# A trunk of attention, recurrence and experts: pass count loaded in VectorE's loop, low parts moved to GpSimd, one pair's low parts behind a norm

## The chip, the cores and the metric

The kernel runs on one core of a Trainium2 chip, as one program. TensorE multiplies, VectorE (DVE) and ScalarE (ACT) work element by element, GpSimd (POOL) does small work and some transfers, and SyncE (SP) issues the weight transfers. The metric is the device time of one execution in microseconds.

## The reference

Two decoder layers on 256 tokens of width 1024, all in float32. Layer 0 mixes the tokens with 16-head latent attention (query rank 384, key and value rank 256) and ends with a dense SwiGLU of width 3584. Layer 1 mixes them with a gated linear recurrence and ends with 8 SwiGLU experts, of which each token uses its best two. In front of each part stands an RMS norm, and one behind the last. Cut to what the change touches:

```python
o = softmax(mask(q @ k.T * scale)) @ v        # 16 heads, 2 blocks of 128 queries
h = h + o @ w_o                               # output projection, 1024 x 1024
...
top_val, top_idx = lax.top_k(logits, 2)       # router of 8 experts
y = sum(gate * swiglu(x, w_gate[e], w_up[e], w_down[e]) for the two experts e)
h = rmsnorm(h + y, norm_final)
```

## The kernel before

The program writes one stream of instructions for each engine, in an order fixed by hand, and joins them by semaphores. An engine works its own stream in order, so an instruction that waits holds all behind it.

**Split products.** Up to the recurrence, a matrix product is three TensorE products: each operand is a high part (rounded, in `w_hi`) and a low part (the rest, in `w_lo`), and high times high, low times high and high times low are summed (`product`, lines 424 to 426). Weights come in units of 128 x 2048 into six slots. For each unit ScalarE makes the high parts (`split_hi`, line 398) and another engine subtracts them from the raw weights (`split_lo`, line 404: two inputs and one output in SBUF). The output projection of the attention has four units, `W_O` to `W_O + 3`; TensorE multiplies by them at the end of the heads. In the dense layer GpSimd makes the low parts of one slot in six, one unit in each step.

**The heads.** Scores, softmax and values of the 16 heads are software-pipelined: a loop over `i` writes, on each engine, the stages of several heads. TensorE transposes head `i` (line 1234), multiplies the scores of head `i - 1` (1245, 1246), transposes the probabilities of head `i - 4` (1255) and multiplies pairs of heads by the values (1270, 1274). Score product `h` waits for the maxima of head `h - 2`, since two banks alternate. VectorE does in step `i`: the norm of head `i - 3` (`normalize`, lines 1892 to 1894: a reciprocal and two multiplications in SBUF), the maxima of head `i - 1` (`maxima`, 1883, one operand in PSUM and one in SBUF, and at the end a 128 x 2 multiplication in SBUF, 1886, which raises `max_ready`), in odd steps from 7 on the low parts of a pair of heads (`o_low`, 1899), and in steps 1 and 4 a copy of keys and values (`kv_copy`, 1871 and 1872). In step 1 it also makes the low parts of unit `W_O + 3`, between the maxima of head 0 and a copy. ScalarE copies transposed heads and probabilities (791), makes the exponentials (880) and the high parts of the pairs. GpSimd's last work before the heads end is two copies of rotated keys (711); then it waits for `heads_over`.

**The experts.** The router's plan gives a number of passes over the experts, 1 to 3 by how many tokens the fullest expert has; with these inputs it is 1. VectorE computes it into `n_pass_i` (line 2197, raising `plan_ready`), and each engine loads it into a register and loops `n_pass` times over the experts. TensorE gathers the first expert's tokens (1506) and runs some filler products (1132), VectorE copies them from PSUM in two halves (`xg_copy`, 2212), and TensorE begins the expert's products (1500) when the first half is there. A loop body is entered once before the count is compared at its end.

Of the kernel before, what the change touches and what calls it, by code (L numbers as in the profile page):

```python
# [21 lines left out]
def trunk(nc, x, positions, norm_mix, norm_ffn, norm_final, mla_w_in, mla_q_norm, mla_kv_norm,  # L22
# [10 lines left out]
    HEADS, V = 16, 64  # L33
# [14 lines left out]
    with ExitStack() as ctx:  # L48
        def sb(stack, name, shape, dt):
            return stack.enter_context(nc.sbuf_tensor(name, shape, dt))  # L50

        def sem(name):
            return ctx.enter_context(nc.semaphore(name))
# [14 lines left out]
        n_pass_i = sb(ctx, "n_pass_i", [1, 1], I32)  # L68
# [137 lines left out]
        def mla_use(n):  # L206
            return n % SLOTS, n // SLOTS + 1
# [101 lines left out]
        plan_ready = sem("plan_ready")  # L309
# [44 lines left out]
        W_IN, W_UQ, W_UKV, W_O = 0, 3, 6, 8  # L354
# [45 lines left out]
        def split_lo(eng, use, width=UNIT):  # L400

            s, n = use
            eng.wait_ge(hi_done[s], n)
            eng.tensor_tensor(w_lo[:, s, 0:width], raw[:, s, 0:width], w_hi[:, s, 0:width].bitcast(F32),  # L404
                              ALU.subtract).then_inc(lo_done[s], 1)
# [228 lines left out]
        def _(pool):  # L634
# [75 lines left out]
            for t in range(TT):  # L710
                pool.tensor_copy(k[:, t, :, NOPE:QK],
                                 latent[:, t, QR + KVR:LAT].unsqueeze(1).broadcast_to([P, HEADS, ROPE])
                                 ).then_inc(qk_ready, 1)

            pool.wait_ge(heads_over, 1)
            gain(2, gain_ffn[:], norm_ffn[0])
# [41 lines left out]
            n_pass = pool.value_load(n_pass_i[0:1, 0:1], min_val=1, max_val=3)  # L758
# [948 lines left out]
        def _(dve):  # L1707
# [3 lines left out]
            def link(ins):  # L1711

                links[0] += 1
                ins.then_inc(link_s, 1)
                dve.wait_ge(link_s, links[0])
                return ins
# [147 lines left out]
            def kv_copy(n):  # L1864
                t, b = KV_ORDER[n]
                if n == len(KV_ORDER) - 1:
                    dve.wait_ge(used[mla_use(W_O - 1)[0]], mla_use(W_O - 1)[1])
                else:
                    dve.wait_ge(kv_ps, n + 1)
                src = psum[:, KV_BANKS[t][b]].rearrange("p (h c) -> p h c", h=4)  # L1870
                dve.tensor_copy(k[:, t, 4 * b:4 * b + 4, 0:NOPE], src[:, :, 0:NOPE]).then_inc(kv_copied_v, 1)
                dve.tensor_copy(v[:, t, 4 * b * V:4 * (b + 1) * V].rearrange("p (h c) -> p h c", h=4),
                                src[:, :, NOPE:NOPE + V]).then_inc(kv_copied_v, 1)


            def maxima(h):

                b = h % 4
                dve.wait_ge(score_ps, h + 1)
                if h >= 4:  # L1880
                    dve.wait_ge(probsT_ps, h - 3)
                for r, (c0, c1) in enumerate([(0, P), (P, 3 * P)]):
                    link(dve.tensor_tensor_reduce(probs[:, b, c0:c1], psum[:, 2 + h % 2, c0:c1],  # L1883
                                                  mask[:, 2 * P - (c1 - c0):2 * P], 1.0,
                                                  -BIG, ALU.add, ALU.max, mx[:, 2 * b + r:2 * b + r + 1]))
                dve.tensor_scalar(nmx[:, 2 * b:2 * b + 2], mx[:, 2 * b:2 * b + 2], -SCALE, None,
                                  ALU.mult).then_inc(max_ready, 1)

            def normalize(h):
                b = h % 4  # L1890
                dve.wait_ge(exp_ready, 2 * h + 2)
                link(dve.reciprocal(inv[:, 2 * b:2 * b + 2], tot[:, 2 * b:2 * b + 2]))
                link(dve.tensor_scalar(probs[:, b, 0:P], probs[:, b, 0:P], inv[:, 2 * b:2 * b + 1], None, ALU.mult))
                dve.tensor_scalar(probs[:, b, P:3 * P], probs[:, b, P:3 * P], inv[:, 2 * b + 1:2 * b + 2], None,
                                  ALU.mult).then_inc(probs_ready, 1)

            def o_low(g):
                dve.wait_ge(o_hi, g + 1)
                dve.tensor_tensor(xTl_mla[:, g, :], psum[:, 6 + g % 2, 0:T], xTh_mla[:, g, :].bitcast(F32),
                                  ALU.subtract).then_inc(o_lo, 1)  # L1900

            for i in range(HEADS + 7):
                if 0 <= i - 3 < HEADS:
                    normalize(i - 3)
                if i == 4:
                    kv_copy(KV_SCALAR + 1)
                if 0 <= i - 1 < HEADS:
                    maxima(i - 1)
                if i == 1:
                    split_lo(dve, mla_use(W_O + 3))  # L1910
                    kv_copy(KV_SCALAR)
                if i >= 7 and i % 2 == 1:
                    o_low((i - 7) // 2)

            dve.wait_ge(o_ps, HEADS // 2)
# [281 lines left out]
            dve.scalar_tensor_tensor(out=n_pass_i[:], in0=rs[0:1, 6, 0:1], scalar=2 * FULL, in1=rs[0:1, 6, 1:2],  # L2197
                                     op0=ALU.is_gt, op1=ALU.add).then_inc(plan_ready, 1)

            dve.wait_ge(plan_ready, 1)  # L2200
            n_pass = dve.value_load(n_pass_i[0:1, 0:1], min_val=1, max_val=3)

            def last_one_hot():
                for t in range(TT):
# [3 lines left out]
            def xg_copy(p):  # L2208

                for h in range(2):  # L2210
                    dve.wait_ge(xg_ps, 2 * p + h + 1)
                    dve.tensor_copy(xg[:, 4 * h:4 * h + 4, :], psum[:, BANK_T[h], 0:4 * SLOT_TOKENS].rearrange(  # L2212
                        "p (a b) -> p a b", b=SLOT_TOKENS)).then_inc((xg_half, xg_v)[h], 1)
# [57 lines left out]
            def choice_difference(p):  # L2271

                then(dve.tensor_scalar(rt[:, 2], rt[:, 5], 0.0, None, ALU.is_equal), p)
                then(dve.tensor_scalar(rt[:, 4], rt[:, 5], 1.0, None, ALU.is_equal), p)
                then(dve.tensor_tensor(rt[:, 3], rt[:, 4], rt[:, 2], ALU.subtract), p)
                then(dve.tensor_tensor(rt[:, 1], rt[:, 3], rt[:, 0], ALU.mult), p)
                then(dve.tensor_reduce(rs[:, 2], rt[:, 1], AX, ALU.add), p)
                dve.wait_ge(rstd_ready, MOE_ROOTS + TT)
                dve.tensor_tensor(rs[:, 2], rs[:, 2], rstd[:, 0:TT], ALU.mult).then_inc(top_diff, 1)
# [40 lines left out]
            def sums(n):  # L2320

                dve.wait_ge(main_ready, n * 6 + 6)
                dve.wait_ge(freed, n * UNITS + leaves((None, STEPS - 1, 0)))
                for d in range(2):
                    half_sum(d)
# [14 lines left out]
            def expert(p, e, e_next, to_xg, first=False, last=False):  # L2340
                n = p * E + e
                for m in range(4):
                    if m == 1 and not first:

                        dve.wait_ge(y_stored, p * 16 * (E - 1) + e * 16 + 48)
                        sums(n - 1)
                    if m == 1 and first:
                        choice_difference(p)
                        find_rows(p)
                    if m == 2 and first:  # L2350
                        gates(p)
                    silu(n, m)
                    if m == 3 and not last:
                        transpose_tokens_of(p, e_next, to_xg).then_inc(xg_v, 1)
                    if m == 3 and last:
                        add_rows(p)
                    for h in range(WIDTH[m]):
                        times_up(n, m, h, first)
                        transpose_hidden(n, m, h)
                    if m == 0 and last:  # L2360
                        last_one_hot()
                        transpose_onehot(p)

            with dve.Fori(0, n_pass) as p:
                xg_copy(p)
                expert(p, 0, 1, xg_odd, first=True)
                with dve.Fori(0, (E - 2) // 2) as h:
                    expert(p, h * 2 + 1, h * 2 + 2, xg)
                    expert(p, h * 2 + 2, h * 2 + 3, xg_odd)
                expert(p, E - 1, None, None, last=True)  # L2370

                dve.wait_ge(ohT_ready, p + 1)
                dve.tensor_scalar(key[:], key[:], -FULL, None, ALU.add).then_inc(pass_over, 1)
                dve.wait_ge(pass_over, p + 1)
                for t in range(TT):
                    first_one_hot(t)

                dve.wait_ge(y_stored, p * 16 * (E - 1) + (64 + 16 * (E - 1)))
                last_sums(p * E + (E - 1), p)
                dve.wait_ge(added, p * 8 + 8)  # L2380
                for i, (d, t) in enumerate([(d, t) for d in range(2) for t in range(TT)]):
                    add_result(p, i, t, d)
                dve.wait_ge(added, p * 8 + 12)
# [37 lines left out]
```

## Time and profile before

| | us |
|---|---|
| median of 3 runs | 1317.88 |
| lowest and highest run | 1317.78, 1318.0 |
| the profiled execution | 1318.05 |
| its span, first to last instruction | 1316.2 |
| TensorE busy in the span | 1305.8 |
| VectorE busy | 642.5 |
| ScalarE busy | 283.2 |
| GpSimd busy | 86.9 |

The span is what the trace covers; the execution's own time is 1.85 us longer. All times of the trace are microseconds from the start of the span. A matmul's end is modelled, so that consecutive matmuls overlap in the rows. "Busy" leaves out register work, branches and waits; in the chain of waits the sequencers' own work stands under names such as DVEq.

### The profile page before, as it was taken

The numbers are of one execution on the slowest core, as the hardware profiler recorded it, in microseconds if no ns is written. First come the engines' busy times: TensorE is split into PE (matmuls) and PEld (weight loads), VectorE is DVE, ScalarE is ACT, GpSimd is POOL, SyncE is SP. The second block draws the span as 40 slices with busy tenths as digits, with TensorE's granted clock in tenths as the row PEclk, the third lists the DMA queues.
The fourth block names the chain that finished last, engine by engine and source line by source line (L and its number), as shares of the span: only waits on it lengthen the run. The fifth ranks groups of instructions, "written<-read, shape, count | busy, mean of one in ns | idle before, by whom it ended". The sixth has DMA issues, their size and how long they took to land.

```text
span 1316.2 us, 25501 instructions
## 1 busy us (share of the span) xinstructions
PE 1305.8 (99%) x10922; PEld 768.1 (58%) x10922; DVE 642.5 (49%) x1458; ACT 283.2 (22%) x424; POOL 86.9 (7%) x114
## 2 busy tenths in 40 slices
PE   9999999999999999999999999999999999999998
PEld 5778888888896544444444444444444444444444
DVE  5978666666776253432533523323353353342436
ACT  4874333333584100010010010001001001000102
POOL 2401111111001100000000000000000000000100
PEclk9999999999999999999999999999999999999999
DMA  7815555556467899999999999999999999999992
GB/s 278 306 61 179 193 191 191 191 191 203 153 250 307 314 412 403 420 410 413 420 420 405 418 420 408 419 412 408 408 420 409 407 420 419 406 400 420 419 415 90
DMA packets 124227, 441.92 MB, mean 336 GB/s; under 512 B 7294, under 2 KB 17600, under 8 KB 109536
## 3 DMA queue, kind: packets, MB, share of 16 engines
q1 hardware_dynamic: 119488, 424.57, 81.9%
q0 software_dynamic: 4624, 15.87, 3.3%
q8 instruction: 82, 1.34, 0.4%
q14 instruction: 17, 0.14, 0.0%
q10 hardware_dynamic: 16, 0.00, 0.0%
HBM read 430.84 MB, written 9.57 MB: 335 GB/s over the span
## 4 chain that ended last, share of the span: by engine, by line
PE 95%; DVE 2%; ACT 1%; DMA 1%; issue 0%; SPq 0%; DVEq 0%; POOL 0%
PE psum L1500 66%; PE psum L424 8%; PE psum L426 8%; PE psum L425 8%; DMA raw<-in_mla_w_uq 1%; PE psum L1473 1%; DVE w_lo L404 1%; PE psum L1506 0%; ACT res L880 0%; PE psum L1147 0%; PE psum L1348 0%; ACT gain_mla L791 0%; PE psum L440 0%; DVE res L1883 0%; ACT early L791 0%
## 5 line engine op out<-in xcount | busy, mean ns | idle before, releaser
L1500 PE MATMUL psum<-raw_more,hT 128*32 128x512 f32 x1656 | 535.7, 592 | 0.0
L1500 PE MATMUL psum<-raw,hT 128*32 128x512 f32 x1032 | 334.8, 592 | 0.0
L1500 PE MATMUL psum<-raw_more,xg_odd 128*32 128x512 f32 x1680 | 245.4, 592 | 0.0
L1500 PE MATMUL psum<-raw_more,xg 128*32 128x512 f32 x1704 | 241.8, 592 | 0.7 <-DVE xg L2212 0.7
L1500 PEld LDWEIGHTS psum<-raw_more,hT 128*32 128x32 f32 x1656 | 146.8, 109 | 122.6 <-issue 122.6
L2248 DVE STREAM_TRANSPOSE hT<-hid 32x128 f32<-32x128 f32 x672 | 204.9, 305 | 10.3
L2238 DVE SCALAR_TENSOR_TENSOR hid<-hid,psum 96x512 f32<-96x512 f32 x55 | 37.6, 684 | 303.3 <-PE psum L1500 302.5
L1092 ACT ACTIVATE hid<-psum 96x1024 f32<-96x1024 f32 (+1 forms) x32 | 29.2, 912 | 664.8 <-PE psum L1500 475.8
L1500 PE MATMUL psum<-raw,xg_odd 128*32 128x512 f32 x1008 | 147.7, 592 | 0.0
L1500 PE MATMUL psum<-raw,xg 128*32 128x512 f32 x984 | 144.2, 592 | 0.0
L1500 PEld LDWEIGHTS psum<-raw,hT 128*32 128x32 f32 x1032 | 91.1, 109 | 76.0 <-issue 75.8
L404 DVE TENSOR_TENSOR w_lo<-raw,w_hi 128x2048 fp32r<-128x2048 f32 (+1 forms) x53 | 119.6, 2276 | 30.6 <-ACT w_hi L398 30.5
L2225 DVE SCALAR_TENSOR_TENSOR hid<-hid,psum 96x1024 f32<-96x1024 f32 (+1 forms) x32 | 34.7, 1084 | 201.8 <-ACT hid L1092 201.8
L1500 PEld LDWEIGHTS psum<-raw_more,xg 128*32 128x32 f32 x1704 | 83.4, 110 | 83.5 <-issue 83.5
L1500 PEld LDWEIGHTS psum<-raw_more,xg_odd 128*32 128x32 f32 x1680 | 84.5, 110 | 77.9 <-issue 77.9
L398 ACT ACTIVATE w_hi<-raw 128x2048 fp32r<-128x2048 f32 (+1 forms) x60 | 111.4, 1889 | 19.4 <-PE psum L426 16.7
L424 PE MATMUL psum<-w_hi,xTh_ffn 128*128 128x512 f32 x224 | 87.3, 390 | 0.0
L426 PE MATMUL psum<-w_hi,xTl_ffn 128*128 128x512 f32 x224 | 87.2, 389 | 0.0
L425 PE MATMUL psum<-w_lo,xTh_ffn 128*128 128x512 f32 x224 | 87.2, 389 | 0.0
L1500 PEld LDWEIGHTS psum<-raw,xg_odd 128*32 128x32 f32 x1008 | 50.7, 110 | 46.8 <-issue 46.8
L1500 PEld LDWEIGHTS psum<-raw,xg 128*32 128x32 f32 x984 | 49.5, 110 | 47.9 <-issue 47.9
L791 ACT ACTIVATE y_main<-psum 32x512 f32<-32x512 f32 x48 | 28.4, 592 | 145.1 <-PE psum L1500 145.1
(318 smaller groups left out, 1343.7 us busy)
## 6 DMA issues: line engine op xcount, KB each, us to landing
raw_more<-in_moe_w_gate SPq DMA_DIRECT2D x71, 1024.0 KB, 16.2
raw_more<-in_moe_w_up SPq DMA_DIRECT2D x70, 1024.0 KB, 15.8
raw_more<-in_moe_w_down SPq DMA_DIRECT2D x69, 1024.0 KB, 16.8
raw<-in_moe_w_down SPq DMA_DIRECT2D x43, 1024.0 KB, 16.8
raw<-in_moe_w_up SPq DMA_DIRECT2D x42, 1024.0 KB, 16.2
raw<-in_moe_w_gate SPq DMA_DIRECT2D x41, 1024.0 KB, 17.2
raw<-in_ffn_w_gate SPq DMA_DIRECT2D x14, 1024.0 KB, 5.1
raw<-in_ffn_w_up SPq DMA_DIRECT2D x14, 1024.0 KB, 5.5
```

The lines of the kernel that those rows point to most:

```text
L398: act.activation(w_hi[:, s, 0:width], raw[:, s, 0:width], ACT.Copy).then_inc(hi_done[s], 1)
L404: eng.tensor_tensor(w_lo[:, s, 0:width], raw[:, s, 0:width], w_hi[:, s, 0:width].bitcast(F32), ALU.subtract).then_inc(lo_done[s], 1)
L424: pe.matmul(out_ap, sh, mh, start=first, stop=False, **lone)
L425: pe.matmul(out_ap, sh, ml, start=False, stop=False, **lone)
L426: mm = pe.matmul(out_ap, sl, mh, start=False, stop=last, **lone)
L791: return act.activation(dst, src, ACT.Copy)
L1092: act.activation(hid[:, 0:WIDTH[m] * BANK].rearrange("p (a b) -> p a b", b=BANK), psum[SLOT_ROWS, 0:WIDTH[m]], ACT.Tanh, scale=0.5).then_i ...
L1473: mm = pe.matmul(psum[rows_q, 2 * t + b], states[:, a, c0:c0 + 32], unit(raw, s, D)[:, a % 2, b * BANK:(b + 1) * BANK], start=a == 0, stop ...
L1500: return pe.matmul(psum[rows_q, bank, cols], stationary, moving, start=start, stop=stop, tile_position=(0, rows_q.start), skip_group_check ...
L2225: dve.scalar_tensor_tensor(out=h, in0=h, scalar=1.0, in1=psum[SLOT_ROWS, 0:WIDTH[m]], op0=ALU.add, op1=ALU.mult).then_inc(m_mid, 1)
L2238: dve.scalar_tensor_tensor(out=hid[:, cols], in0=hid[:, cols], scalar=0.5, in1=psum[SLOT_ROWS, BANK_U[h]], op0=ALU.mult, op1=ALU.mult).the ...
L2248: ins = dve.transpose(hT[QUARTERS[to], H_BUF[j], :, QUARTERS[b]].rearrange("p (h r) s -> p h r s", r=2), hid[QUARTERS[b], h * BANK:(h + 1) ...
```

## The change

It has three parts. VectorE no longer loads the pass count ahead of its loop; the wait for the plan and the load stand inside the loop, behind the two token copies, and the range check of the value is left out. The low parts of unit `W_O + 3` are made by GpSimd behind its key copies and not by VectorE in step 1. And `o_low` of pair 4, until now at the end of step 15, stands in step 16 between the norm of head 13 and the maxima of head 15; the other pairs stay where they were.

```diff
--- before.py
+++ after.py
@@ -711,6 +711,8 @@
                 pool.tensor_copy(k[:, t, :, NOPE:QK],
                                  latent[:, t, QR + KVR:LAT].unsqueeze(1).broadcast_to([P, HEADS, ROPE])
                                  ).then_inc(qk_ready, 1)
+
+            split_lo(pool, mla_use(W_O + 3))
 
             pool.wait_ge(heads_over, 1)
             gain(2, gain_ffn[:], norm_ffn[0])
@@ -1902,14 +1904,17 @@
             for i in range(HEADS + 7):
                 if 0 <= i - 3 < HEADS:
                     normalize(i - 3)
+                if i == HEADS:
+                    o_low((HEADS - 1 - 7) // 2)
                 if i == 4:
                     kv_copy(KV_SCALAR + 1)
                 if 0 <= i - 1 < HEADS:
                     maxima(i - 1)
                 if i == 1:
-                    split_lo(dve, mla_use(W_O + 3))
                     kv_copy(KV_SCALAR)
-                if i >= 7 and i % 2 == 1:
+                if 7 <= i < HEADS - 1 and i % 2 == 1:
+                    o_low((i - 7) // 2)
+                if i > HEADS and i % 2 == 1:
                     o_low((i - 7) // 2)
 
             dve.wait_ge(o_ps, HEADS // 2)
@@ -2197,8 +2202,7 @@
             dve.scalar_tensor_tensor(out=n_pass_i[:], in0=rs[0:1, 6, 0:1], scalar=2 * FULL, in1=rs[0:1, 6, 1:2],
                                      op0=ALU.is_gt, op1=ALU.add).then_inc(plan_ready, 1)
 
-            dve.wait_ge(plan_ready, 1)
-            n_pass = dve.value_load(n_pass_i[0:1, 0:1], min_val=1, max_val=3)
+            pass_count = dve.alloc_register("pass_count")
 
             def last_one_hot():
                 for t in range(TT):
@@ -2361,8 +2365,10 @@
                         last_one_hot()
                         transpose_onehot(p)
 
-            with dve.Fori(0, n_pass) as p:
+            with dve.Fori(0, pass_count) as p:
                 xg_copy(p)
+                dve.wait_ge(plan_ready, 1)
+                dve.reg_load(pass_count, n_pass_i[0:1, 0:1])
                 expert(p, 0, 1, xg_odd, first=True)
                 with dve.Fori(0, (E - 2) // 2) as h:
                     expert(p, h * 2 + 1, h * 2 + 2, xg)
```

## Rows read from the trace of the kernel before

**Rows 1.** The page, busy time of TensorE; and its granted clock in 40 slices.

```profile
PE 1305.8 (99%) x10922; PEld 768.1 (58%) x10922; DVE 642.5 (49%) x1458; ACT 283.2 (22%) x424; POOL 86.9 (7%) x114
...
PEclk9999999999999999999999999999999999999999
```

**Rows 2.** The waits of TensorE: for whom; us in total, times, longest us.

```profile
PE psum L1245 <- DVE res L1886: 0.9, 1, 0.9
...
PE psum L1500 <- DVE xg L2212: 0.7, 1, 0.7
```

**Rows 3.** The chain of waits, 52 to 62 us: start, us, what.

```profile
54.22 2.19 DVE w_lo L404
...
58.11 0.46 PE psum L1245 x2
```

**Rows 4.** The chain of waits, 78 to 92 us.

```profile
83.61 0.42 DVE xTl_mla L1899
...
84.88 0.55 PE psum L1255 x3
```

**Rows 5.** The chain of waits, 428 to 446 us.

```profile
435.90 1.15 DVEq L2201
...
437.61 0.57 DVE xg L2212
438.18 0.34 issue
```

**Rows 6.** The timeline of VectorE: start, us, instruction, count; idle time before it.

```profile
46.04 0.85 DVE L1855 TENSOR_TENSOR q<-gain_mla 128x256 f32<-128x256 f32 x1
...
54.05 0.17 DVE L1886 TENSOR_SCALAR res<-res 128x2 f32<-128x2 f32 x1
...
56.33 0.42 DVE L1871 COPY k<-psum 128x256 f32<-128x256 f32 x1
...
57.00 0.28 DVE L1883 CUSTOM_DVE_ANT_0 res<-psum,mask 128x128 f32<-128x128 f32 x1
...
57.32 0.42 DVE L1883 CUSTOM_DVE_ANT_0 res<-psum,mask 128x256 f32<-128x256 f32 x1
...
58.06 0.29 DVE L1893 TENSOR_SCALAR res<-res 128x128 f32<-128x128 f32 x1
58.38 0.35 DVE L1894 TENSOR_SCALAR res<-res 128x256 f32<-128x256 f32 x1
...
86.12 0.35 DVE L1894 TENSOR_SCALAR res<-res 128x256 f32<-128x256 f32 x1
...
156.08 0.69 DVE L1971 SCALAR_TENSOR_TENSOR hid_f<-hid_f,psum 128x512 f32<-128x512 f32 x1 [4.12 <-PE psum L426]
```

**Rows 7.** The timeline of GpSimd (POOL).

```profile
36.13 2.33 POOL L697 TENSOR_TENSOR res<-k,res 128x16 f32<-128x16 f32 x1
...
45.81 0.81 POOL L696 TENSOR_TENSOR k<-q,trig 128x256 f32<-128x256 f32 x1
...
153.12 4.62 POOL L404 TENSOR_TENSOR w_lo<-raw,w_hi 128x2048 fp32r<-128x2048 f32 x1 [26.19 <-ACT w_hi L398]
```

**Rows 8.** The timeline of ScalarE (ACT).

```profile
51.79 1.91 ACT L398 ACTIVATE w_hi<-raw 128x2048 fp32r<-128x2048 f32 x1
...
151.13 1.91 ACT L398 ACTIVATE w_hi<-raw 128x2048 fp32r<-128x2048 f32 x1
```

**Rows 9.** The timeline of TensorE (PE).

```profile
86.66 0.49 PE L1255 MATMUL psum<-ident,res 128*128 128x128 f32 x3
...
435.47 2.02 PE L1506 MATMUL psum<-onehot,xn_moe 128*128 128x96 f32 x16
437.38 0.39 PE L1132 MATMUL psum<-zeros 128*128 128x128 bf16 x4
```

**Rows 10.** Line 1697, TensorE's loop: duration ns min/median/max, first and last start us.

```profile
L1697 PEldq FUSED_REGOPS  x1: 41/41/41, 437.5 to 437.5; - x1
```

**Rows 11.** The timeline of VectorE in the first expert.

```profile
453.55 1.22 DVE L2225 SCALAR_TENSOR_TENSOR hid<-hid,psum 96x1024 f32<-96x1024 f32 x1 [14.92 <-ACT hid L1092]
```

## The prediction

> **What bounds the kernel now.** I read the page's busy times first [rows 1]: TensorE is busy for 99% of the span, so an edit elsewhere counts only where TensorE waits for it. The list of TensorE's waits comes next. It is short, and two entries touch the change [rows 2]: 0.9 us for a VectorE operation of line 1886, and 0.7 us for the token copies of line 2212. The chain of waits then says what stands behind each. In the attention it runs through VectorE from the low parts of the last output-weight unit (54.22, 2.19 us) by the value copies and the second head's maxima to the score product of head 3 at 58.11 [rows 3]. At the end of the heads it runs through `o_low(4)` (83.61, 0.42 us) and the norm of head 13 to TensorE at 84.88, and from there on TensorE works without a gap [rows 4]. Before the expert loop it runs through VectorE's load of the pass count (435.90, 1.15 us) and the first token copy (437.61) to the first expert product, 0.34 us behind the copy [rows 5]. These are the three places edited; the rest is TensorE's own stream, which moves as a block.
>
> **Part A, the pass count.** Removed ahead of the copies: the load, 1.15 us, and the range check behind it, some 0.3 us. The copies then wait for the gather products alone. These 16 records, starting at 435.47, take 2.02 us, to 437.49 [rows 9], so the half that the first copy needs is done about 436.5; the copy takes 0.57 us [rows 5] and ends about 437.1 instead of 438.18. Next late is TensorE itself: its four filler products reach to 437.77 [rows 9], and its own load of the count and loop entry occupy its sequencer until 437.5 [rows 10]. The 0.34 us of issue between copy and product I take as sequencer work on waits; placed behind 437.54 it gives a start at 437.88 instead of 438.52, a gain of 0.64. The most it can be is the wait itself, 0.74 us [rows 5, 9]; the least is nothing. I take 0.65. The second copy is due 0.57 us later, and the product that needs it stands four weight tiles behind the first, so it does not hold. Inside the loop the wait and the load come behind the copies; queued behind them is the first `silu`, which starts only at 453.55 after 14.92 us of idleness [rows 11]. So the load costs nothing there; without that cover it would cost its 1.15 us again. No DMA is issued or moved, and the counts of the other queues are as they were.
>
> **Part B, the low parts on GpSimd.** VectorE loses one operation, 2.19 us on the chain. What that can give is limited by TensorE's wait behind it, 0.9 us [rows 2, 3]: with the maxima of head 1 early, the score product of head 3 starts when the transposes in front of it are done. On GpSimd the same operation takes 4.62 us [rows 7]. GpSimd is idle then and waits for ScalarE's high parts, which end at 51.79 + 1.91 = 53.70 [rows 8]. In the dense layer GpSimd starts 0.08 us behind such an end (151.13 + 1.91 against 153.12 [rows 7, 8]), so here it runs from 53.78 to 58.40. The consumer is TensorE in the output projection, after 90 us, and the slot's next load is a dense weight with tens of microseconds to spare; neither waits. GpSimd's next operation is a load of a gain behind the end of the heads.
>
> The cost is in what VectorE can do in those 4.62 us. The trace shows the two engines shutting each other out: a GpSimd operation of 16 columns took 2.33 us at 36.13, beside VectorE's subtractions, where one of 256 columns takes 0.81, and VectorE's operation of line 1855 took 0.85 us at 46.04, ending 0.27 us behind GpSimd's operation, which ran until 46.62 [rows 7, 6]. Both sides wait for a whole instruction of the other. Not every VectorE instruction is caught: at 156.08, inside a GpSimd split of 4.62 us, one with an operand in PSUM took its ordinary 0.69 us [rows 6]. So the maxima and value copies, which read PSUM, go on. The open question is the single-input operation from SBUF to SBUF. `normalize` takes 0.29 us for 128 columns and 0.35 for 256, so 128 more cost some 0.07 us, where the maxima's cost 0.14 (0.28 and 0.42) [rows 6]: it handles two elements in the time of one, as if it read and wrote by two paths. The operation that ends each head's maxima, line 1886, is of the same kind, with two columns. It is issued at 54.05 [rows 6], 0.27 us behind GpSimd's start. If it is shut out, it ends some 0.1 us behind 58.40, and everything queued behind it on VectorE waits with it: ScalarE's exponentials of head 0, TensorE's score product of head 2, the value copies, the maxima of head 1. From the first value copy at 56.33 to TensorE's start at 58.11 it is 1.78 us now [rows 3, 6]; from 58.48 that leads to 60.26, 2.15 us later than before. TensorE's order behind that point (score product, an up-projection, fillers, transposes) has no gap to absorb it. Bounds: from a gain of 0.9 (nothing is shut out) to a loss of 2.15. I take the loss of 2.15, because the nearest operation of this kind in the trace runs at the doubled rate and both kinds of exclusion that can be seen are total.
>
> The Trainium skill ("SBUF — State Buffer", Who interferes with whom) states that VectorE's second port pair is GpSimd's too, locked for a whole instruction, and that `tensor_scalar` takes it when it runs in a two-port mode; the condition ("VectorE: DVE Perf Modes", Mode 2×_2P) is both sides in SBUF and an even outermost dimension, and no least size is named. By that rule the two-column operation is held and the sum is the one below; if only operations long enough to profit took the port, it would be the first rival. No row here shows the small operation beside a GpSimd instruction.
>
> **Part C, the order at the last heads.** `o_low(4)` moves from in front of the norm of head 13 to behind it. The chain loses 0.42 us there, and TensorE's wait would let it pass. But VectorE's total up to the norm of head 14 is unchanged: it ends at 86.12 + 0.35 = 86.47 [rows 6]. TensorE's transposes of that head started at 86.66, behind a product and not behind VectorE [rows 9]; 0.42 us earlier they would now wait for the norm, until about 86.5. So 0.15 us is left. Ends: 0 and 0.42. The product that reads `o_low(4)` comes two heads later. I take 0.15.
>
> **Sum.** +2.15 - 0.65 - 0.15 = +1.35 us. The profiled execution took 1318.05 us (span 1316.2 and 1.85 around it), so 1319.4; it lies 0.17 above the median of the runs, 1317.88, so in the terms of that median 1319.2.
>
> **Rivals.**
> 1. The two-column operation passes, only the norms are shut out. Head 0's norm, started at 58.06 before, gets its turn at 58.40, and VectorE's queue is 0.34 us later than now behind it, which eats part of the 0.9 us: B is -0.7 (ends -0.9 and -0.55), the sum -1.5, the time 1316.4. For it: a two-column operation gains nothing from the second path. Against it: the norms' rate.
> 2. Nothing single-input is shut out. B is -0.9, the sum with A and C -1.7 to -2.1, the time 1316.0. For it: no row shows such an operation held.
> 3. The first line-1886 operation slips in ahead of GpSimd's start, the second is held to 58.40 and ends at about 58.57, so that TensorE starts near 58.7 instead of 58.11: B +0.6, the sum -0.2, the time 1317.7. It needs GpSimd 0.27 us later than the dense layer's rows say.
> 4. The other side, slower by a measurable amount: with VectorE held, TensorE stands idle most of 56 to 60 us, and its granted clock, 1.00 in every slice of the page [rows 1], falls to its lower level of 1.2 GHz. TensorE's work behind the hold would take twice its time until the clock is back; if that lasts as long as the hold, 4.35 us from 54.05 to 58.40, half of it is lost, 2.2 us, and the time 1321.4. It decides from 1.3 us upward. Against it: there is a score product and a set of transposes inside the hold.
> That the count is loaded too late to do its work in the loop can't be: it is read only at the end of the pass.
>
> **How the numbers follow.** What a measurement of this kernel can tell from no change is about 0.2%, 2.6 us. Likeliest case 0.50, 1319.2, with its own range 1318.6 to 1320.0 (A between 0 and 0.74, C between 0 and 0.42). Rival 1: 0.17. Rival 2: 0.17. Rival 3: 0.08. Rival 4: 0.08. The range from 1315.6 to 1320.2 takes in all but rival 4 and the ends. Faster than 1315.2 needs all three gains at their ends and more: 0.04. Slower than 1320.5 is rival 4 and the case's own upper end: 0.09. The rest, 0.87, is within 0.2%.
>
> **What the changed profile would show.** GpSimd's split at 53.8 for 4.6 us; the first line-1886 operation as one of some 4.4 us instead of 0.17, or, by rival 1, line 1893 at 56.7 with some 1.7 us and line 1886 short; TensorE's score product of head 3 at 60.3 (57.2 by rivals 1 and 2). No `TENSOR_LOAD` of VectorE between the gather and the first copy, and TensorE's wait there gone or under 0.1 us. `o_low` of pair 4 behind the norm of head 13, TensorE's wait for line 1894 shorter. The prediction is wrong if VectorE keeps its short operations beside GpSimd's split, or if TensorE's clock falls.

## The result, and the profile after

The changed kernel takes 1320.39 us (median of 18 runs, 1319.32 to 1322.05), the kernel before 1318.01 (18 runs, 1317.18 to 1321.86). The ratio is 1.0019, with a 95% interval of 1.0012 to 1.0025: 2.4 us slower. The forecast was 1319.2 with a range up to 1320.2, so the time lies just outside of it. The profiled execution took 1319.79 us, its span is 1317.9.

The first rows are of the page of the changed kernel; the one on TensorE's clock shows nothing, since a slice is 33 us wide and a 9 stands for anything from 0.90 up.

```profile
PE 1308.6 (99%) x10922; PEld 770.2 (58%) x10922; DVE 642.6 (49%) x1457; ACT 283.5 (22%) x424; POOL 91.5 (7%) x115
...
PEclk9999999999999999999999999999999999999999
```

TensorE's waits in the changed kernel (us in total, times, longest us), to be read against [rows 2]. Line numbers have moved by two: 1888 is now the end of the maxima, 1247 the score product, 1257 the transposes of the probabilities.

```profile
PE psum L1247 <- DVE res L1888: 2.3, 1, 2.3
...
PE psum L1257 <- DVE res L1896: 0.3, 1, 0.3
PE psum L1502 <- issue: 0.2, 1, 0.2
```

TensorE's wait for the maxima was 0.9 us, at head 3's score product for the maxima of head 1. It is now 2.3 us, and stands one head earlier: at head 2's score product, for the maxima of head 0. The wait for the token copies is gone; 0.2 us of issue stand in its place. Why the first grew is in the timelines of GpSimd and VectorE:

```profile
53.00 4.52 POOL L404 TENSOR_TENSOR w_lo<-raw,w_hi 128x2048 fp32r<-128x2048 f32 x1 [4.79 <-ACT w_hi L398]
```

```profile
53.26 4.29 DVE L1888 TENSOR_SCALAR res<-res 128x2 f32<-128x2 f32 x1
57.46 0.41 DVE L1873 COPY k<-psum 128x256 f32<-128x256 f32 x1
...
58.91 0.17 DVE L1888 TENSOR_SCALAR res<-res 128x2 f32<-128x2 f32 x1
...
59.18 0.29 DVE L1895 TENSOR_SCALAR res<-res 128x128 f32<-128x128 f32 x1
```

GpSimd's split starts at 53.00 and ends at 57.52. VectorE issues the two-column operation at 53.26 and completes it at 57.55: 4.29 us for work that took 0.17 [rows 6]. The value copies behind it, with their input in PSUM, start at once afterwards, and the norm of head 0 (59.18, 0.29 us) finds GpSimd done. TensorE in the same stretch:

```profile
54.97 0.38 PE L1236 MATMUL psum<-ident,k 128*96 128x128 f32 x2
57.69 0.46 PE L1247 MATMUL psum<-gain_mla 96*128 96x128 f32 x2 [2.34 <-DVE res L1888]
...
59.23 0.77 PE L1247 MATMUL psum<-gain_mla 96*128 96x128 f32 x2
...
60.28 0.99 PE L424 MATMUL psum<-w_hi,xTh_mla 128*128 128x512 f32 x1
61.07 0.63 PE L425 MATMUL psum<-w_lo,xTh_mla 128*128 128x512 f32 x1
...
62.21 0.40 PE L425 MATMUL psum<-w_lo,xTh_mla 128*128 128x512 f32 x1
...
63.03 0.50 PE L1257 MATMUL psum<-ident,res 128*128 128x128 f32 x3
```

It is idle from 55.35 to 57.69. Then the products themselves are slow: the one at 60.28 takes 0.99 us and the next 0.63, against 0.40 for the same kind at 62.21. The table by microsecond says why (length, busy us of each engine, then the granted clock, then DMA):

```profile
56.00:57.00 1.00, 0.00 (x0) 0.00 (x0) 1.00 (x1) 0.00 (x0) 1.00 (x1) 1.00 0.95 377
...
58.00:59.00 1.00, 1.00 (x8) 0.76 (x6) 0.93 (x7) 1.00 (x4) 0.00 (x0) 0.81 0.89 123
59.00:60.00 1.00, 1.00 (x5) 0.81 (x4) 0.93 (x6) 0.94 (x5) 0.00 (x0) 0.50 0.63 221
...
61.00:62.00 1.00, 1.00 (x4) 0.73 (x3) 0.47 (x2) 0.00 (x0) 0.00 (x0) 0.50 0.83 340
62.00:63.00 1.00, 1.00 (x10) 0.68 (x9) 0.12 (x1) 0.00 (x0) 0.00 (x0) 0.99 0.06 16
```

The granted clock is 0.81 in the slice from 58 us, 0.50 (TensorE's lower level, 1.2 GHz) from 59 to 62, and 0.99 in the next. It fell after TensorE had been idle for the whole of the microsecond from 56 and most of the two beside it, and was back at 62, with TensorE at work since 57.69. In the trace of the kernel before, with 0.87 us of idleness in this place, the granted clock is 1.00 in each microsecond from 54 to 64. Nor is one trace alone in this: the mean clock of the span is below 1.000 in 17 of the 18 runs of the changed kernel, and in 2 of the 78 runs of the kernel before that were made beside the experiments. In this trace the stage comes 0.79 us earlier than in that of before (the two-column operation is issued at 53.26 and not at 54.05), so the stage is best measured from that issue: head 3's score product follows 5.97 us behind it (before 4.06), and the first transposes of probabilities (63.03) 3.80 us behind the score product (before 60.57 - 58.11 = 2.46). The hold costs 1.91 us, the slow clock 1.34.

The chain of waits at the last heads answers to [rows 4], and before the experts to [rows 5]; VectorE's timeline there stands below.

```profile
88.45 0.36 DVE res L1896
...
88.86 0.55 PE psum L1257 x3
```

```profile
437.83 1.90 PE psum L1508 x16
439.73 0.29 PE psum L1134 x4
440.01 0.23 issue
440.24 5.77 PE psum L1502 x50
```

```profile
438.87 0.56 DVE L2216 COPY xg<-psum 128x384 f32<-128x384 f32 x1 [0.78 <-PE psum L1508]
439.77 0.56 DVE L2216 COPY xg<-psum 128x384 f32<-128x384 f32 x1 [0.34 <-PE psum L1508]
455.27 1.22 DVE L2229 SCALAR_TENSOR_TENSOR hid<-hid,psum 96x1024 f32<-96x1024 f32 x1 [14.95 <-ACT hid L1094]
```

The norm of head 14 now ends the wait at 88.86, as forecast. Before the experts VectorE's load has left the chain: it runs through gather, fillers and 0.23 us of issue to the product at 440.24. The copies start at 438.87 and 439.77, each as its half of the gather is ready, and VectorE's next operation comes at 455.27, so the load behind them (1.14 us at 439.8) is hidden.

### The profile page after: what moved, and what is told of

It is laid out like the page before. It is cut to its first block, busy times and chain, and to the rows that moved or that the text cites. A ratio compares the mean times of both kernels' runs of the same rounds, so it can differ in the third digit from the quotient of the medians.

```text
span 1317.9 us, 25499 instructions
## 1 busy us (share of the span) xinstructions
PE 1308.6 (99%) x10922; PEld 770.2 (58%) x10922; DVE 642.6 (49%) x1457; ACT 283.5 (22%) x424; POOL 91.5 (7%) x115
## 3 DMA queue, kind: packets, MB, share of 16 engines
q8 instruction: 82, 1.34, 0.4%
## 4 chain that ended last, share of the span: by engine, by line
PE 96%; DVE 2%; ACT 1%; issue 0%; DMA 0%; POOL 0%; POOLq 0%; DVEq 0%
PE psum L1502 66%; PE psum L424 8%; PE psum L425 8%; PE psum L426 8%; PE psum L1149 1%; PE psum L1475 1%; PE psum L1508 1%; DMA q<-in_positions 0%; DVE w_lo L404 0%; DVE res L1888 0%; ACT res L882 0%; POOL k L653 0%; PE psum L1350 0%; ACT gain_mla L793 0%; PE psum L440 0%
```

## The experiments

All are compared with the kernel before by 8 to 11 executions of theirs and 15 to 33 of its own; the interval of each ratio is about 0.0009 to either side, so that it tells 1.2 us but not 0.2. Parts of that size are read from the traces, by the distances between five marks that no noise of the start-up reaches: the issue of the first two-column operation (M), the first transposes of probabilities (T), the last 256-column products of the heads by the values (V), the first of the last 16 gather products (G) and the first expert product (X). V to G is 345.66 to 345.68 us in all eleven traces, and X to the end 877.64 to 877.73. A distance comes from one trace of each kernel, but kernels with the same code in a stretch agree there: T-V is 29.19 to 29.22 us in before, A alone and B alone, and M-T 6.50 to 6.52 us wherever VectorE kept the split in step 1. Only G-X scatters more, 2.38 to 2.54 us in the eight kernels with part A. The mark M itself moves from 52.93 to 54.74 us from trace to trace, and what moves it is left out of the sums.

```
kernel        median us  ratio   M-T   T-V    G-X   sum against before
before        1317.9     1       6.52  29.22  3.05
changed       1320.39    1.0019  9.77  29.01  2.54  +2.53
A alone       1317.81    0.9998  6.51  29.21  2.46  -0.61
B alone       1321.46    1.0028  9.76  29.19  3.05  +3.21
C alone       1317.66    1.0000  6.51  29.03  3.04  -0.21
A and C       1316.91    0.9997  6.50  29.03  2.54  -0.72
fillers       1319.14    1.0008  8.45  29.03  2.38  +1.07
one column    1316.01    0.9986  5.42  29.25  2.48  -1.64
odd norm      1316.95    0.9992  5.42  30.03  2.49  -0.85
pieces        1316.53    0.9994  5.86  29.02  2.44  -1.47
late split    1316.11    0.9984  5.41  29.03  2.38  -1.97
```

(Each ratio is to runs of the kernel before made beside those of the other; these had medians of 1317.66 to 1318.21 us, and the table shows a middle one. A ratio differs from the quotient of two medians by up to 0.0004.)

**One part at a time.** My theory was that the parts add up and that all of the loss is B's: hold and clock. The rival put some of it on A or C, or on their sum.

```diff
 # A alone
-            dve.wait_ge(plan_ready, 1)
-            n_pass = dve.value_load(n_pass_i[0:1, 0:1], min_val=1, max_val=3)
+            pass_count = dve.alloc_register("pass_count")
...
-            with dve.Fori(0, n_pass) as p:
+            with dve.Fori(0, pass_count) as p:
                 xg_copy(p)
+                dve.wait_ge(plan_ready, 1)
+                dve.reg_load(pass_count, n_pass_i[0:1, 0:1])
```

> Part A alone (count loaded in the loop), the rest as before. Theory (the three parts add up, and A is worth what TensorE waited for the copies): the first expert product starts 0.64 us earlier behind the gather (before: 438.52 - 435.47 = 3.05 us from the first gather product to it; here 2.4), and the time is 0.05% below before. Rival (the move of code costs something of its own in the loop, and is part of the loss of the whole change): the same distance is 3.0 us or the expert part is longer than before, ratio 1.000 or above.

The distance G-X fell from 3.05 to 2.46 us, 0.59 us, and the expert part is as long as before. The ratio is 0.9998 (0.9989 to 1.0007). The size is the theory's; the ratio by itself is also compatible with nothing.

```diff
 # B alone
+            split_lo(pool, mla_use(W_O + 3))
             pool.wait_ge(heads_over, 1)
...
-                    split_lo(dve, mla_use(W_O + 3))
                     kv_copy(KV_SCALAR)
```

> Part B alone (low parts of the last output-weight unit on GpSimd), the rest as before. Theory (the loss is all B's: a two-column operation held for 4.3 us, about 2.0 us, and the clock that falls behind it, about 1.3 us): the two-column operation takes 4.3 us, the granted clock is below 1.00 between 56 and 64 us, ratio 1.0022 to 1.0028, about 3.2 us above before. Rival (only the hold is B's, the rest is from A or C or their sum): ratio 1.0010 to 1.0016, clock 1.00.

VectorE's operation and the granted clock in this kernel:

```profile
53.45 4.28 DVE L1888 TENSOR_SCALAR res<-res 128x2 f32<-128x2 f32 x1
```

```profile
56.00:60.00 4.00, 2.12 (x11) 1.71 (x12) 3.86 (x12) 2.17 (x8) 1.71 (x1) 0.85 0.64 201
60.00:64.00 4.00, 4.00 (x23) 3.21 (x23) 2.50 (x13) 1.02 (x4) 0.00 (x0) 0.72 0.52 210
```

The hold is there (4.28 us) and so is the clock (0.85 and 0.72), the ratio is 1.0028 (1.0018 to 1.0039), and the distances give 3.21 us. The rival falls.

```diff
 # C alone
                     normalize(i - 3)
+                if i == HEADS:
+                    o_low((HEADS - 1 - 7) // 2)
...
-                if i >= 7 and i % 2 == 1:
+                if 7 <= i < HEADS - 1 and i % 2 == 1:
                     o_low((i - 7) // 2)
+                if i > HEADS and i % 2 == 1:
+                    o_low((i - 7) // 2)
```

> Part C alone (o_low of pair 4 behind the norm of head 13), the rest as before. Theory: TensorE's wait for the norm of head 13 (0.77 us) shrinks to about 0.35, 0.2 us is kept behind the norm of head 14, ratio 0.9998, not to be told from 1. Rival (it is worth the 0.42 us that leaves the chain): the transposes behind the norm of head 14 start 0.4 us earlier, ratio 0.9997. The trace tells them apart, the ratio doesn't.

TensorE's wait for the norm of head 13 is 0.3 us instead of 0.8, and T-V is 0.19 us shorter: the norm of head 14 takes the rest, as the theory has it. The rival's 0.4 us is not there. The ratio, 1.0000 (0.9991 to 1.0009), tells nothing.

> The change without part B. Theory (gains of A and C stand by themselves and add): 0.64 + 0.2 = 0.85 us below before, ratio 0.9993. Rival (they show only together with B, or are eaten): ratio 1.0000.

The distances give 0.72 us less, the ratio is 0.9997 (0.9988 to 1.0006). The sum of A alone (0.61) and C alone (0.21) is 0.82; the 0.1 us between is within what G-X varies by from trace to trace with the same code (2.38 to 2.54).

**Hold and clock apart.** TensorE is kept busy inside the hold, with products whose results nobody reads.

```diff
+                if i == 3:
+                    pe.wait_ge(kv_copied_a, 8)
+                    keep_busy(40, 4)
                 if 0 <= i - 1 < HEADS:
                     scores(i - 1)
```

> The whole change, with 40 filler products on TensorE (2.3 us of them) in front of the score product of head 2, where it otherwise waits 2.3 us for the held operation. Theory (two losses, hold and clock): the hold stays (two-column operation 4.3 us, score product of head 3 as late as in the changed kernel), the granted clock stays 1.00 in 56 to 64 us, and the transposes of the first probabilities start 1.3 us earlier than in the changed kernel; ratio to before 1.0009. Rival (the whole loss is the hold, the clock is a by-product that costs nothing): ratio as of the changed kernel, 1.0019, with a clock of 1.00.

VectorE's operation, TensorE's timeline and the granted clock:

```profile
53.55 4.32 DVE L1891 TENSOR_SCALAR res<-res 128x2 f32<-128x2 f32 x1
```

```profile
55.48 2.40 PE L1134 MATMUL psum<-zeros 128*128 128x128 bf16 x40
...
59.54 0.46 PE L1247 MATMUL psum<-gain_mla 96*128 96x128 f32 x2 [0.20 <-DVE res L1891]
...
60.09 0.59 PE L424 MATMUL psum<-w_hi,xTh_mla 128*128 128x512 f32 x1
```

```profile
59.00:60.00 1.00, 0.80 (x7) 0.57 (x5) 0.89 (x6) 0.93 (x4) 0.00 (x0) 1.00 0.61 152
...
61.00:62.00 1.00, 1.00 (x10) 0.70 (x9) 0.90 (x5) 0.00 (x0) 0.00 (x0) 1.00 1.01 418
```

The hold is as long as before, 4.32 us, and head 3's score product comes 5.99 us behind its issue (5.97 in the changed kernel). But the clock stays at 1.00, the first up-projection product takes 0.59 us and not 0.99, and the first transposes follow the score product by 2.46 us, as in the kernel before. M-T is 1.32 us shorter than in the changed kernel, and the mean clock is 1.000 in all 11 runs. The ratio falls from 1.0019 to 1.0008 (0.9999 to 1.0017); the two intervals overlap, so the size rests on the traces. The slow clock is a loss of its own, not a by-product.

**What is shut out.** Here the two-column operation is replaced for heads 0 and 1.

```diff
+                if h < 2:
+                    for c in range(2 * b, 2 * b + 2):
+                        ins = dve.tensor_scalar(nmx[:, c:c + 1], mx[:, c:c + 1], -SCALE, None, ALU.mult)
+                    ins.then_inc(max_ready, 1)
+                    return
                 dve.tensor_scalar(nmx[:, 2 * b:2 * b + 2], mx[:, 2 * b:2 * b + 2], -SCALE, None,
                                   ALU.mult).then_inc(max_ready, 1)
```

> The whole change, but for heads 0 and 1 the operation that ends the maxima is written as two operations of one column each. Theory (a one-input operation from SBUF to SBUF is shut out by GpSimd's instruction if it has an even number of columns, so that it uses two paths): the one-column operations take 0.15 us inside GpSimd's split, the clock stays 1.00; the norm of head 0 (128 columns) is held instead until the split ends, by up to 1.7 us; ratio to before 0.9988 (about 1.5 us below). Rival (whatever VectorE reads and writes in SBUF with one input is shut out): the first one-column operation takes 4.3 us, and the ratio is that of the change, 1.0019.

```profile
53.99 0.22 DVE L1890 TENSOR_SCALAR res<-res 128x1 f32<-128x1 f32 x2
...
56.48 0.21 DVE L1890 TENSOR_SCALAR res<-res 128x1 f32<-128x1 f32 x2
56.61 0.15 DVE L1899 RECIPROCAL res<-res 128x2 f32<-128x2 f32 x1
56.80 1.56 DVE L1900 TENSOR_SCALAR res<-res 128x128 f32<-128x128 f32 x1
```

```profile
53.73 4.55 POOL L404 TENSOR_TENSOR w_lo<-raw,w_hi 128x2048 fp32r<-128x2048 f32 x1 [4.79 <-ACT w_hi L398]
```

GpSimd's split runs from 53.73 to 58.28. The one-column operations inside it take 0.22 us a pair, and the first operation of the norm, with 128 columns, is held until 58.36. The ratio is 0.9986 (0.9977 to 0.9995) and the clock 1.00: with one operation written in two, the loss of 2.5 us is a gain of 1.6. The held norm costs TensorE some 0.2 us (T-V is 29.25 against 29.03). The rival, that every one-input operation is shut out, falls. It falls by another row too: the reciprocal at 56.61 has one input, works from SBUF to SBUF and has two columns, and it took its ordinary 0.15 us inside the split (0.16 without one). So two columns are not enough for a hold; the kind of operation matters, and all that were held are of the kind `tensor_scalar`. But my theory had a second half, that the number of columns must be even. It was tried on the norm:

```diff
+                if h == 0:
+                    for c0, c1 in ((0, P - 1), (P - 1, P), (P, 3 * P - 1), (3 * P - 1, 3 * P)):
+                        r = 2 * b + (c0 >= P)
+                        ins = link(dve.tensor_scalar(probs[:, b, c0:c1], probs[:, b, c0:c1], inv[:, r:r + 1], None,
+                                                     ALU.mult))
+                    dve.sem_inc(probs_ready, 1)
+                    return
```

> As the run with one-column operations for heads 0 and 1, and the norm of head 0 besides in pieces of 127, 1, 255 and 1 columns instead of 128 and 256. Theory (what decides is whether the number of columns is even, not how many there are): no piece is held inside GpSimd's split, the piece of 127 columns takes about 0.28 us and the one of 255 about 0.42 (one element at a time) instead of 1.56 and 0.35; TensorE's wait for the norms of heads 0 and 1 is gone; ratio 0.9985 to 0.9988, since the hold of that norm cost TensorE only 0.2 us. Rival (size decides: a short operation passes, a long one is held): the piece of 127 columns takes 1.5 us.

Groups of VectorE's instructions, 56 to 60.3 us (count, busy us, mean ns):

```profile
L1903 DVE TENSOR_SCALAR res<-res 128x127 f32<-128x127 f32 x1 | 1.6, 1560 | 0.0
...
L1903 DVE TENSOR_SCALAR res<-res 128x1 f32<-128x1 f32 x2 | 0.4, 214 | 0.1
L1903 DVE TENSOR_SCALAR res<-res 128x255 f32<-128x255 f32 x1 | 0.4, 354 | 0.0
```

The piece of 127 columns took 1.56 us, to the end of the split, as 128 did, so the theory's second half falls. The piece of 255, issued when GpSimd was done, took 0.35 us, as 256 columns do and not the 0.42 of one element at a time. Odd widths too use the doubled rate, and are held. The rival of that run, that size decides, does not stand in its place: two columns are held in the changed kernel. What the runs show is that a `tensor_scalar` of one column passes, and those of 2, 127 and 128 columns are held. The run itself is 0.8 us worse than with one-column operations, since the four linked pieces are longer than two.

**GpSimd's work in pieces.**

```diff
-            split_lo(pool, mla_use(W_O + 3))
+            s_last, n_last = mla_use(W_O + 3)
+            pool.wait_ge(hi_done[s_last], n_last)
+            for c in range(8):
+                part = slice(c * UNIT // 8, (c + 1) * UNIT // 8)
+                ins = pool.tensor_tensor(w_lo[:, s_last, part], raw[:, s_last, part],
+                                         w_hi[:, s_last, part].bitcast(F32), ALU.subtract)
+            ins.then_inc(lo_done[s_last], 1)
```

> The whole change, with GpSimd's split in 8 instructions of 256 columns (about 0.58 us each) instead of one of 2048. Theory (an instruction is held for one whole instruction of the other engine): the two-column operation waits at most 0.6 us, TensorE's wait behind it goes, the clock stays 1.00, GpSimd's split as a whole is longer than 4.6 us; ratio 0.9987 to 0.9995. Rival (GpSimd keeps VectorE out as long as it has work queued): the two-column operation takes 4.3 us again, ratio 1.0019.

```profile
52.93 0.51 DVE L1894 TENSOR_SCALAR res<-res 128x2 f32<-128x2 f32 x1
...
55.43 0.74 DVE L1894 TENSOR_SCALAR res<-res 128x2 f32<-128x2 f32 x1
...
56.28 0.64 DVE L1901 TENSOR_SCALAR res<-res 128x128 f32<-128x128 f32 x1
```

```profile
52.68 5.60 POOL L719 TENSOR_TENSOR w_lo<-raw,w_hi 128x256 fp32r<-128x256 f32 x8 [4.80 <-ACT w_hi L398]
```

A piece takes 0.70 us (5.60 / 8), and VectorE's operations wait for at most one: they take 0.51 and 0.74 us with two columns (0.17 alone) and 0.64 with 128 (0.29 alone), 0.34 to 0.57 us more than alone. GpSimd needs 5.60 us instead of 4.5. The clock stays at 1.00, M-T falls to 5.86 us, and the ratio is 0.9994 (0.9985 to 1.0003). A hold lasts one instruction of the other engine, not its queue.

**Without GpSimd.** If TensorE waits only at head 3's score product, the unit's low parts can be made wherever VectorE is idle. The edit is shown against the kernel with parts A and C.

```diff
-                    split_lo(dve, mla_use(W_O + 3))
                     kv_copy(KV_SCALAR)
+                if i == HEADS + 2:
+                    split_lo(dve, mla_use(W_O + 3))
...
-            for s in range(SLOTS):
+            for s in range(SLOTS - 1):
                 load(sp, (s, FFN_BASE + 1), ffn_v[s // 2][0, s % 2, 0])
             sp.wait_ge(heads_over, 1)
             sp.dma_start(res[:], x[0].rearrange("(t p) d -> p t d", p=P)).then_inc(x_again, 16)
+            s = SLOTS - 1
+            load(sp, (s, FFN_BASE + 1), ffn_v[s // 2][0, s % 2, 0])
```

> Parts A and C, and the low parts of the last unit on VectorE behind the norm of head 15, where VectorE idles; the dense weight of that slot is loaded behind the second load of x. Theory (TensorE waits 0.9 us for VectorE at the score product of head 3 and nothing else needs this unit before the end of the heads): 0.9 + 0.64 + 0.2 = 1.75 us below before, ratio 0.9987. Rival (the 2.2 us come back at the end of the heads, where the output projection waits for the unit or for the low parts behind it): ratio 0.9993 or above, with a wait of TensorE in the output projection.

```profile
86.67 2.28 DVE L404 TENSOR_TENSOR w_lo<-raw,w_hi 128x2048 fp32r<-128x2048 f32 x1
88.87 0.42 DVE L1901 TENSOR_TENSOR xTl_mla<-psum,xTh_mla 128x256 fp32r<-128x256 f32 x1
```

```profile
PE psum L1257 <- DVE res L1896: 0.3, 1, 0.3
```

The split stands at 86.67, and TensorE has no listed wait for it or for the low parts at 88.87; the one wait listed at the heads' end is that for the norm of head 13. M-T is 1.11 us shorter than before, the sum of the distances 1.97 us, and the ratio 0.9984 (0.9975 to 0.9993). It is below both kernels by more than the intervals. By the distances it is the best of all that ran, 0.33 us ahead of the kernel with one-column operations; the ratios, 0.9984 and 0.9986, can't tell the two apart.

## Why the prediction was wrong

**The step that failed** is the price of the hold: the sum takes it as time alone, +2.15 us, and puts the fall of TensorE's clock behind it at nothing. I had that fall as rival 4, as something else that might happen, with a chance of 0.08 and the argument that a score product and a set of transposes inside the hold speak against it. They do lie inside the hold, but at its start. The transposes were done at 55.35, the next score product waited for the held operation, and TensorE was idle for 2.34 us. The fall of the clock came with the hold: it showed in the changed kernel and in B alone, and went when TensorE was kept busy. Its size was over-priced where it was named (2.2 us against 1.34) and left out of the sum where it belonged. With it, the sum is +1.35 + 1.34 = +2.7, and the measured medians are 2.4 apart. The other terms were each a little off, and in part cancel: the hold cost 0.24 us less than forecast, A gave 0.14 less and C 0.06 more. The prediction also read a clock of 1.00 out of the page's digits [rows 1], which say only 0.90 or more; the mean clock of that run, 1.000, bears it out.

**Part B, the hold.** Right in place and mechanism: GpSimd's start behind ScalarE's high parts, the two-column operation of 4.3 us (forecast "some 4.4"), everything else queued behind it. The hold's price was 1.91 us against 2.15, since GpSimd needed 4.52 us and not 4.62, and head 3's score product came 1.71 us behind its end (57.52 to 59.23) and not 1.86. The end to the other side was also right: where the operation is not held (one column, late split), TensorE's whole wait goes, 1.03 us at the score product (forecast 0.9) and 1.1 at the first transposes.

The Trainium skill's rule ("SBUF — State Buffer", Who interferes with whom), that VectorE in a two-port mode and GpSimd lock each other out for a whole instruction, agrees with these runs on VectorE's side: 4.29 us in the changed kernel, at most one piece of 0.7 us (5.60 / 8) in the run with pieces. I gave the condition for that mode ("VectorE: DVE Perf Modes", Mode 2×_2P) short: the page also allows an odd dimension if it is equal on both sides. The 127 columns that were held agree with the page, not with my theory of even widths.

**Part A.** Right: the copies leave the chain, TensorE itself is next late, and the load is free in the loop. The chain shows the fillers to 440.01 and 0.23 us of issue behind them, where the prediction had set 0.34 us behind the sequencer's work on the loop. The gain was 0.51 us in the changed kernel and 0.59 alone, against 0.65.

**Part C.** Right: the norm of head 14 takes back half of it; 0.2 us against 0.15.

**What stays open.** Why G-X differs by up to 0.16 us between kernels with the same code there was not tried, nor was an operation with three columns. That operations other than `tensor_scalar` pass rests on one kind, the reciprocal of two columns. What else of TensorE's idleness brings its clock down was not tried either: the runs have the gap of 2.3 us, or have it filled or gone.

## What to carry to other kernels

Before work is moved to GpSimd, list what VectorE issues while it runs, down to the smallest operation. A two-column multiplication with input and output in SBUF stood for the length of GpSimd's whole instruction, and all that TensorE waited for stood behind it. Price a hold twice, once as time and once as TensorE's idleness: where a hold leaves TensorE idle, look at the granted clock behind it in slices of a microsecond. And before an engine is relieved, see whether it has an idle place later that the consumer can wait for: that was worth as much here as the best kernel with a second engine, and by the traces 0.33 us more.

## What the runs showed of the hardware

- VectorE's `tensor_scalar` operations from SBUF to SBUF with 2, 127 and 128 columns were held by a GpSimd subtraction that read SBUF, to its end (4.29, 1.56 and 1.56 us; alone 0.17 with 2 columns and 0.29 with 128). With one column they passed (0.22 us for two of them), and so did a reciprocal of two columns (0.15 us).
- Cutting GpSimd's instruction into 8 cut the hold to 0.57 us at most, and took GpSimd 5.60 us instead of 4.52.
- TensorE, idle from 55.35 to 57.69 us, then had a granted clock of 0.50 from 59 to 62 us (0.81 in the microsecond before), and lost 1.34 us by it, though the mean clock of the span reads 0.999.
